# The order of the attention units in a two-block kernel: kinds in turn, or one kind after the other

## The reference: what is computed

```python
def diff_attention(q, k, v, lam_params, subln_g, lambda_init):      # branch a, 4 heads
    ...
        s = jnp.einsum('bqhcd,bkhcd->bhcqk', qi, k) * scale          # two maps per head, c = 0, 1, of depth 64
        s = s - slopes * dist;  s = jnp.where(dist >= 0, s, -jnp.inf)
        p = jax.nn.softmax(s, axis=-1)
        a = p[:, :, 0] - lam * p[:, :, 1]                            # one matrix of weights from the two
        return jnp.einsum('bhqk,bkhe->bqhe', a, v)                   # values of width 128

def nsa_attention(q, kv, gates, ...):                                # branch b, 8 heads, depth 64
    ...
    o = gates[..., 0:1] * o_cmp + gates[..., 1:2] * o_slc + gates[..., 2:3] * o_win
```

## Time and profile before

| | |
|---|---|
| median of 3 runs | 2982.13 us (2981.83 to 2985.3) |
| the profiled execution | 2982.13 us, its span 2980.4 us |
| TensorE busy | 2851.0 us, 96% of the span |
| VectorE busy | 1566.0 us, 53% |
| GpSimd busy | 1383.8 us, 46% |
| ScalarE busy | 1009.8 us, 34% |
| the chain that ended last | PE 79%, issue 7%, DVE 6%, POOL 5%, ACT 2% |
| the attention units of the second block | 866 to 1022 us of the span |

### The profile page before, as it was taken

One profiled execution on the slowest core, in us unless ns is written; L12 is line 12 of the kernel. 1 busy time (PEld: TensorE's weight loads), 2 busy tenths in 40 slices (PEclk: granted clock), 3 DMA queues, 4 the chain that ended last, 5 costly groups with the idle time before them and its releaser, 6 DMA issues.

```text
span 2980.4 us, 35638 instructions
## 1 busy us (share of the span) xinstructions
PE 2851.0 (96%) x13610; PEld 2332.0 (78%) x13610; DVE 1566.0 (53%) x2401; ACT 1009.8 (34%) x1519; POOL 1383.8 (46%) x537
## 2 busy tenths in 40 slices
PE   7988999999989989999989999999999999999997
PEld 5745888887876678878878888888888888888885
DVE  3477652442247516469967978530004555555554
ACT  3255322232136433354333333332223222222222
POOL 4691454544310034525457777764445444444441
PEclk9978999999989999999999999999999999999999
DMA  3200222224210023322335665564465656666651
GB/s 129 71 0 29 85 95 90 99 88 152 99 43 1 1 85 113 113 71 78 118 97 165 202 183 158 169 204 162 148 202 189 193 190 194 190 190 196 197 190 64
DMA packets 222321, 375.93 MB, mean 126 GB/s; under 512 B 11152, under 2 KB 142608, under 8 KB 211216
## 3 DMA queue, kind: packets, MB, share of 16 engines
q1 hardware_dynamic: 222224, 374.68, 38.7%
HBM read 305.43 MB, written 69.21 MB: 126 GB/s over the span
## 4 chain that ended last, share of the span: by engine, by line
PE 79%; issue 7%; DVE 6%; POOL 5%; ACT 2%; DMA 1%; POOLq 0%; SPq 0%; DVEq 0%; ACTq 0%
PE bank L258 15%; PE bank L260 15%; PE bank L259 15%; PE bank L1925 8%; PE bank L1926 8%; PE bank L1927 8%; POOL rows_b L1724 4%; DVE cacc L454 2%; PE bank L1216 2%; PE bank L1905 1%; PE bank L1187 1%; POOL w_lo L250 1%; PE bank L1196 1%; POOL u_lo L1682 1%; DMA w_raw<-w_small 1%
## 5 line engine op out<-in xcount | busy, mean ns | idle before, releaser
L250 POOL TENSOR_TENSOR w_lo<-w_raw,w_hi 128x2048 fp32r<-128x2048 f32 (+2 forms) x96 | 423.2, 4410 | 711.6 <-ACT w_hi L245 711.4
L2095 DVE TENSOR_TENSOR h_lo<-h_raw,h_hi 128x512 fp32r<-128x512 f32 x128 | 308.9, 2413 | 352.3 <-ACT h_hi L1704 352.3
L1699 POOL TENSOR_TENSOR v_lo<-v_raw,v_hi 128x1024 fp32r<-128x1024 f32 x128 | 307.9, 2406 | 377.5 <-ACT v_hi L1695 377.5
L1682 POOL TENSOR_TENSOR u_lo<-u_raw,u_hi 128x1024 fp32r<-128x1024 f32 x128 | 324.8, 2538 | 339.7 <-ACT u_hi L1676 339.7
L258 PE MATMUL bank<-xh,u_lo 128*128 128x512 f32 x1024 | 404.6, 395 | 0.4 <-POOL u_lo L1682 0.3
L1925 PE MATMUL bank<-h_hi,v_lo 128*128 128x512 f32 x1024 | 399.7, 390 | 4.2 <-DVE h_lo L2095 4.2
L1926 PE MATMUL bank<-h_lo,v_hi 128*128 128x512 f32 x1024 | 399.4, 390 | 0.0
L1927 PE MATMUL bank<-h_hi,v_hi 128*128 128x512 f32 x1024 | 399.3, 390 | 0.0
L259 PE MATMUL bank<-xl,u_hi 128*128 128x512 f32 x1024 | 398.9, 390 | 0.0
L260 PE MATMUL bank<-xh,u_hi 128*128 128x512 f32 x1024 | 398.8, 389 | 0.0
L258 PE MATMUL bank<-xh,w_lo 128*128 128x512 f32 x768 | 305.5, 398 | 29.1 <-POOL w_lo L250 15.4
(11 more groups left out here) (371 smaller groups left out, 4887.5 us busy)
## 6 DMA issues: line engine op xcount, KB each, us to landing
w_raw<-w_small SPq DMA_DIRECT2D x80, 1024.0 KB, 4.9
u_raw<-expert_u SPq DMA_DIRECT2D x128, 512.0 KB, 3.8
v_raw<-expert_v SPq DMA_DIRECT2D x128, 512.0 KB, 5.1
h_scratch<-h_act SPq DMA_DIRECT2D x128, 256.0 KB, 2.2
g_scratch<-stage SPq DMA_DIRECT2D x8, 4096.0 KB, 16.7
h_raw<-h_scratch SPq DMA_DIRECT2D x128, 256.0 KB, 2.7
g_in<-g_scratch SPq DMA_DIRECT2D x64, 512.0 KB, 4.1
w_raw<-w_small SPq DMA_DIRECT2D x8, 768.0 KB, 4.3
```

Of the source, the lines that this page charges most:

```text
L250: pool.tensor_tensor(wl[g % 2][:, :n], raw[g % 2][:, :n], wh[g % 2][:, :n].bitcast(F32), ALU.subtract).then_inc(sem("lo_done"), 1)
L1682: pool.tensor_tensor(u_lo[c % 2][:, :, :], u_raw[c % 4][:, :, :], u_hi[c % 2][:, :, :].bitcast(F32), ALU.subtract)\
L1699: pool.tensor_tensor(v_lo[c % 4][:, :], v_raw[c % 4][:, :], v_hi[c % 4][:, :].bitcast(F32), ALU.subtract)\
L2095: dve.tensor_tensor(h_lo[c % 4][:, :], h_raw[c % 4][:, :], h_hi[c % 4][:, :].bitcast(F32), ALU.subtract)\
```

## The change

The list of units is written in another order: first all 16 units of kind a, head by head, then all 32 of kind b, head by head. `items` and `head_no`, which follow from the order, are written as plain formulas for it. All else in the program is the same text; lines below the change move up by three.

```diff
-        HEADS2 = [x for h in range(DA_H) for x in (("a", h), ("b", h))] + [("b", h) for h in range(DA_H, NSA_H)]
-
-        UNITS = [HEADS2[2 * p + x] + (i,) for p in range(DA_H) for i in range(QT) for x in range(2)]
-        UNITS += [head + (i,) for head in HEADS2[2 * DA_H:] for i in range(QT)]
+        UNITS = [("a", h, i) for h in range(DA_H) for i in range(QT)] + [("b", h, i) for h in range(NSA_H) for i in range(QT)]
+        N_A = DA_H * QT
         NU = len(UNITS)
 
         def items(u):
 
-            first = sum(1 if UNITS[v][0] == "a" else 2 for v in range(u))
-            return [first] if UNITS[u][0] == "a" else [first, first + 1]
+            return [u] if u < N_A else [N_A + 2 * (u - N_A), N_A + 2 * (u - N_A) + 1]
 
         def head_no(u):
-            return HEADS2.index(UNITS[u][:2])
+            return u // QT
```

## The result

The changed kernel is slower: 3002.66 us median (3002.35 to 3005.39, 4 runs) against 2982.49 (2981.83 to 2985.3, 4 runs), a ratio of 1.0069, 95% interval 1.0054 to 1.0085. That is 20.2 us more, where 12 were forecast; the range ended 0.7 short of it. The profiled execution is the quickest of the seven on record: 2999.07 us, its span 2997.3, 16.9 more than before. It is the one that can be taken apart.

The account below looks back on a forecast made before the run. TensorE paced the mixed stretch; a heads alone would be bound by VectorE (9.9 us). First a0's slope to b5's: 9.7 + 33.0 + 0.7 + 12.6 + 59.0 = 115.0 against 102.9, 12.1 more: 2994.2 us, range 2988 to 3002.

Parts of the forecast that it names:

- The steady a head, 11.0: Each a head after the first: VectorE's 9.9 us plus stalls of 0.65 and 0.4; three make 33.0 us.
- The stall before width 384: VectorE waiting for scores before the width-384 maxima of an a head: TensorE's way 2.3 against 1.92, 0.4 us.
- The stall before width 512: VectorE waiting for scores before the width-512 maxima of an a head, 0.65 us.
- W256: VectorE's weights step of an a unit of width 256 (reciprocal, lambda, scale, difference), 1.23 us.
- The way to 512: From the end of VectorE's width-256 maxima through ScalarE's copy and TensorE to the first width-512 maximum, 3.02 us.
- TensorE's a head, 5.7: TensorE's work in one a head: scores 2.4, transposes 1.1, value records 2.2, together 5.7 us.
- the rival that has an a head cost 5.7 to 6.5: Faster: a units together run as tightly as TensorE's own work; four heads give back 8 us, 2974; chance 0.03.
- The first head, 9.7: First a head, slope to next slope: empty queues, TensorE at half clock until about 877.5; 9.7 us.
- b0, 12.6: First b head, behind only a units: 14.76 less twice the rebate of 1.17; 12.6 us, bounds 12 and 14.76.
- b1 to b4, 59.0: The next four b heads at the steady 14.76 us each, 59.0 us.
- The clock, 0.7: Second a head longer by 0.7 us if TensorE's clock rises some us later than before.
- the half clock as a rival: Half clock stays through the a phase: a head 15.5; 3008 for three heads, 2999 for one; chance 0.15.

Follow-up runs that it names:

- e10: Changed kernel without two of the four VectorE instructions of an a unit's weights step, plus the added products of e9: 2987.73 us, ratio 1.0012.
- e9: Changed kernel with 4 added, overwritten TensorE products a head in the pauses of the a phase: 2990.73 us, ratio 1.0022.
- e5: Changed kernel without two of the four VectorE instructions of an a unit's weights step, plus the added products of e1: 2990.36 us, ratio 1.0020.
- e1: Changed kernel with 10 added, overwritten TensorE products a head in the pauses of the a phase: 2993.61 us, ratio 1.0033.
- e4: Changed kernel without two of the four VectorE instructions of an a unit's weights step, no added products, result not the reference's: 2999.73 us, ratio 1.0048.
- e7: Changed kernel with the added products of e1 only from the last a head's second unit to the next head's first unit: 2995.11 us, ratio 1.0039.
- e2: Changed kernel reordered to whole heads in turn, one a, one b, then the remaining four b heads: 3016.8 us, ratio 1.0098.
- e3: Changed kernel reordered to all b heads first, then all a heads: 2999.76 us, ratio 1.0055.
- e11: Kernel before with another mix, two b units then one a unit through all heads, no added products: 2990.09 us, ratio 1.0019.

## Why the prediction was wrong, by its own steps

- **The direction and its cause.** The direction is right. Of the cause, VectorE's 9.9 us a head are the largest part of an a head's 10.55 at full clock, and the mixed order had hidden them. That VectorE alone sets the a head is not so: by e10 the way around is nearly as long.
- **The steady a head, 11.0.** Measured 11.22, 11.04 and 11.91 with dips of the clock, 10.55 at full clock. The stall before width 384 is there, 0.45 where I had 0.4 (e9). The stall before width 512, 0.65, is not there at full clock: VectorE starts that step 0.16 late at most (1.39 from the reciprocal at 897.69 to the maximum at 899.08, against W256 1.23). The way to 512 is what I had, 3.0 (896.08 to 899.08). But the time that VectorE stands before 384 runs for that way as well, so of the 0.65 only 0.65 - 0.4 = 0.25 could be left, and 9.9 + 0.4 + 0.25 is the 10.55 that was measured. Two waits of one ring are not summed.

```profile
896.53 0.56 DVE L1398 CUSTOM_DVE_ANT_0 att_e<-bank,slope_dist 128x384 f32<-128x384 f32 x1 [0.45 <-PE bank L1184]
```

- **TensorE's a head, 5.7.** Too low. I had left out the joins, some twelve a head at about 0.1; in e5 it is nearer 7.5 (TensorE is busy in nearly all of 9.9 us there, with 2.2 of added products in them). In the a phase VectorE was busy 85% of the time and TensorE 78%, part of it at half clock, where I had 90% and not much over 60%. It did not enter the forecast, but the rival that has an a head cost 5.7 to 6.5 rested on it.
- **The first head, 9.7.** Measured 8.6, counted from the same place (1.54 behind the slope's start at 866.07, to 876.18).
- **b0, 12.6.** At full clock 10.73: a b head behind a heads is 3.9 cheaper, not 2.2. In the changed kernel 16.46.
- **b1 to b4, 59.0.** 60.9, because b1 took 16.89. That was one of the signs I had named for the prediction being wrong: b heads that follow each other not at 14.76.
- **The clock, 0.7. This is the step that failed.** Against the full-clock pieces of e1, the profile shows 2.5 us on a1 to a3, 5.7 on b0 and 2.3 on b1, 10.5 in all. The 0.7 that I had put on a1 for a late rise is there (11.22 against 10.55); the falls behind it I had at nothing. By the timed runs the added products of e9 gain 13.7 us (20.2 - 6.5). I had the half clock as a rival at 0.15, but priced it on the a heads, where VectorE hides much of it, and did not ask what stands behind them: b heads bound by TensorE. And my argument against it, 10.2 us idle in 96 at clock 1.00, came from a stretch with more work of TensorE between its pauses. The waits of TensorE before, 878 to 962 us (us in total, times, longest), and after, 881 to 911 us:

```profile
PE bank L1196 <- ACT att_pt L1036: 8.3, 11, 1.1
```

```profile
PE bank L1193 <- DVE att_e L1405: 6.9, 6, 2.0
```

The total is alike; it comes in 30 us instead of 84, and in pauses of up to 2.0 us instead of 1.1. By e4 and e7 the length of the pauses is not what decides.
- **The sum.** Without the clock term my sum was 11.4. With the clock up in the a phase the kernel is 6.5 (e9) or 10.2 (e1) over before, and the stretch is 7.9 or 9.2 over (164.9 and 166.2 against 157.0). Taking the clock's 10.5 from the 17.2 that the profile has between a0 and b5 leaves 6.7. So the order costs some 7 to 10, less than I had it, and the clock some 10 to 14 more. The two errors went opposite ways, and that the forecast still came within 8 us of the measured change is in part luck.

The rule that I had weighed, the Trainium skill, "TensorE: Matmul & The Clock Gate", section "A second HAM failure mode: psum-queue depth-cycling", says that frequent short pauses between groups of matmuls can make the clock swing between its two levels. The trace of the changed kernel agrees: PEclk goes 1.00, 0.50, 1.00, 0.50 between 886 and 912, and four added products a head (e9) end it. The kernel before, with 8.3 us in 11 pauses and the clock at 1.00, shows that short pauses need not do it. No run here tells what part the transposes have in it.

What stays open: what of TensorE's activity the clock goes by; no run here isolates it. The timed executions of the changed kernel are 3.3 to 6.3 us longer than the profiled one, and e2's spread over nearly 16 us. The mean granted clock goes with it (0.971 in the profiled one, 0.969 or 0.970 in the others), which fits dips of another length or number; the places of these dips were not seen.

## What to carry to other kernels

When a reordering leaves TensorE waiting for another engine in a stretch, price two things: that engine's own sum per unit, and what stands behind the stretch, because a clock that has fallen is paid by the next work that TensorE bounds. Waits of one ring of engines are not added up: the time spent in one of them counts for the next. Mixing work heavy on one engine with work heavy on another hides both; before undoing such a mix, add up the second engine's pitches per unit. If the light stretch can't be avoided, a few products in the pauses, written where they are overwritten, are a cheap test of how much of the loss is the clock's: here four a head were enough.

## What was not expected of the hardware

The clock stayed at 0.50 for 20 us, from 911 to 931, while TensorE was busy in 20.00 of 20.00 us (the window row above). In the a phase it was back some 3 us after it fell. The other runs have the same two kinds where nothing was added: where only b units followed the fall, the clock stayed down for 17 to 21 us (e4, and e2 apart from its first fall, which joins the half clock of the start), and where a units followed it, for 3 to 7 us (e3, e4, e7; in the mix of e11 3 us). No run tells why they differ. Added work made the kernel faster: 46 products of 128 by 128 (10 a head and 6 at b0's first unit) by 10 us, 19 of them (4 a head and 3) by 13.7.
